# Neighbourhood bias rows repeated in 512-byte pieces, and the repeat moved behind the small loads of block 0

## The chip, the cores and the metric

One core of a Trainium2 chip runs the whole program. Its engines are TensorE (PE in the rows, PEld for its weight loads), VectorE (DVE), ScalarE (ACT), GpSimd (POOL) and SyncE (SP); 16 DMA engines move the data, fed by queues that the engines fill. The metric is device time of one execution in microseconds. Smaller is better.

## What is computed

Two blocks of layers, one after the other, on 256 tokens of width 1024. The first block has two layers: a mixer (latent attention in layer 0, dilated attention with a relative bias in layer 1), a gated feed-forward net and a gated extra term:

```
for i in range(DEPTH):
    hn = rms_norm(h, g[0])
    y = mla_mixer(...)  or  dilated_mixer(..., rel_bias)
    h = h + rms_norm(y, g[1])
    h = h + rms_norm(swiglu(rms_norm(h, g[2]), ffn_w_in[i], ffn_w_out[i]), g[3])
    h = h + (p[i] @ ple_w_proj[i]) * jax.nn.sigmoid(h @ ple_w_gate[i])
```

The second block has two layers with differential attention, spatial gating, neighbourhood attention and a mixture of 32 experts. The neighbourhood attention adds a bias that depends on how far the key's column is from the query's column, read from a small table `na_rpb` of 8 heads x 15 row distances x 31 column distances for each layer:

```
rpb_c = rpb[:, :, dc_idx]            # dc_idx = key column - query column + 15, clipped
bias = jnp.take(rpb_c, dr_idx, axis=1)
s_win = jnp.where(col_ok, s_win + bias, NEG_INF)
```

## The kernel before

All engines run one long program each and meet at semaphores. What matters here is the stretch from about 137 to 470 us: the end of the latent attention of layer 0, its output product, the residual, and the first feed-forward net.

**Weights.** SP streams the weights of every product in chunks of 1 MB (a few are smaller) into `weight_ring`, which has four slots (L46, L535). A chunk is asked for as soon as the PE has finished with the chunk four places ahead of it. In the products of this stretch each chunk is used in two parts: ScalarE writes a rounded copy ("high", L1236), GpSimd subtracts it from the chunk and writes the rest ("low", L1486, `low_parts`), and the PE multiplies with the high part (L672, L673) and then with the low part (L677).

**GpSimd's queue.** GpSimd also issues the small loads, in the order of its program and into one DMA queue (q0 in the rows). `load` (L1448) waits until VectorE has asked (`misc_ask`) and then issues one transfer; `row` loads a row of 1024 gains to all 128 partitions (`broadcast_row`). Four DMAs of constants, two tables and one store of the padded neighbourhood rows to DRAM (`rpb_rows`, L1464, 120 rows of 127 numbers for each layer) come first. After that it waits for the attention's first turned probabilities and then issues

- L1509, which copies each of 48 rows of 384 numbers 128 times from DRAM to DRAM (`rel_rows_repeated`, 6144 pieces of 1536 bytes, for the dilated attention);
- L1511, which copies each of 240 rows of 127 numbers 64 times (`rpb_rows_repeated`, 15360 pieces of 508 bytes). The neighbourhood attention reads it far later, with a row step of one number less than the row's length, so that each query column gets its row shifted by one (L1551 to L1554, 64 loads of 64 KB);
- the gain row of the first residual (`row(I["norm_g"][0, 1])`).

Then comes `close_block(0, ...)`. It waits for `port_free`, makes the low parts of the output product's four chunks, issues the gain row of the second residual and the tokens' extra input `p_t` as soon as VectorE asks for them, waits for `port_free` again and makes the low parts of the feed-forward weights.

**VectorE** copies the product out (L1958), sums squares (L1710), waits for the gain row (`loaded()`), and scales by it and adds to the residual (L1967, L1968). It asks for the next two loads and turns the normed rows for the feed-forward net (L1738 to L1757, L1727, L1728), behind which it frees the port.

Of the kernel before, what the change touches and what calls it, by code (L numbers as in the profile page):

```python
# [21 lines left out]
DEPTH = 2  # L22
# [14 lines left out]

OFF_KA, OFF_VA, OFF_KC, OFF_VC, OFF_QA, OFF_QC, OFF_ZB, OFF_GATE = 0, 512, 1024, 1536, 2048, 2560, 3072, 4096
GRID_W, NA_COLS, NA_H, RPB_R, RPB_C = 64, 16, 8, 15, 31
RPB_W = 2 * GRID_W - 1  # L40

NE, NGRP, EPG, D_EXP = 32, 4, 8, 512
CAP = 64
# [91 lines left out]
def build_program(nc, I, out):  # L135
    ctx = ExitStack()
    with ctx:
# [10 lines left out]
        def sem(name):  # L148
            return ctx.enter_context(nc.semaphore(name))
# [32 lines left out]
        rel_dram = nc.dram_tensor("rel_rows", [DIL_G * DIL_H, BIAS_LEN], F32, kind="Internal").ap()  # L182
        rpb_skew = nc.dram_tensor("rpb_rows_repeated", [DEPTH * NA_H * RPB_R, GRID_W * RPB_W], F32, kind="Internal").ap()
        skew_dram = nc.dram_tensor("rel_rows_repeated", [DIL_G * DIL_H, P * BIAS_LEN], F32, kind="Internal").ap()
        gate_dram = nc.dram_tensor("gate_rows_out", [DEPTH, 4 * D], F32, kind="Internal").ap()
        rpb_dram = nc.dram_tensor("rpb_rows", [DEPTH, NA_H * RPB_R, RPB_W], F32, kind="Internal").ap()

# [31 lines left out]
        def ar(a, n):  # L219
            return A[:, a:a + n]  # L220
# [63 lines left out]
        skew_out, rpb_out = sem("bias_rows_repeated"), sem("rpb_rows_repeated")  # L284
# [1156 lines left out]
        def _(pool):  # L1441
# [3 lines left out]
            def load(dst, src):  # L1445

                pool.wait_ge(misc_ask, seen.next(misc_ask))
                nc.gpsimd.dma_start(dst, src).then_inc(misc_in[loads[0] % 4], 16)  # L1448
                loads[0] += 1

            def row(src, width=D, at=0):
                load(brow[:, at:at + width], src.partition_broadcast(P))
# [10 lines left out]
            for l in range(DEPTH):  # L1463
                nc.gpsimd.dma_start(rpb_dram[l], A[0:NA_H * RPB_R, l * P:l * P + RPB_W]).then_inc(scratch_out, 16)  # L1464

# [12 lines left out]
            def low_parts(g, only=None):  # L1478

                for n, (_, width) in enumerate(g.chunks):  # L1480
                    if only is not None and n not in only:
                        continue
                    for i, (k0, kn) in enumerate(g.groups):
                        c, s = g.first[n] + i, g.first_split[n] + i
                        pool.wait_ge(high_ready, s + 1)
                        nc.gpsimd.tensor_tensor(slot(c, kn, width, ring_r), slot(c, kn, width),  # L1486
                                                high(s, kn, width), ALU.subtract).then_inc(low_ready, 1)

            def after_turn():

                pool.wait_ge(port_free, seen.next(port_free))

            def close_block(i, g_o):
                after_turn()
                low_parts(g_o)
                row(I["norm_g"][i, 3])
                load(ar(PLE, 512).rearrange("p (k t) -> p k t", k=2), I["p_t"][i].rearrange("(k p) t -> p k t", p=P))
                after_turn()
                low_parts(g_ff_in[i])
                low_parts(g_ff_out[i])  # L1500
                if i == 0:
                    row(I["norm_g"][1, 1])
                after_turn()
                low_parts(g_ple_g[i])
# [3 lines left out]

            nc.gpsimd.dma_start(skew_dram.rearrange("r (q m) -> r q m", m=BIAS_LEN),  # L1509
                                rel_dram.unsqueeze(1).broadcast_to([DIL_G * DIL_H, P, BIAS_LEN])).then_inc(skew_out, 16)  # L1510
            nc.gpsimd.dma_start(rpb_skew.rearrange("r (q m) -> r q m", m=RPB_W),  # L1511
                                rpb_dram.rearrange("l r w -> (l r) w").unsqueeze(1).broadcast_to(
                                    [DEPTH * NA_H * RPB_R, GRID_W, RPB_W])).then_inc(rpb_out, 16)
            row(I["norm_g"][0, 1])
            close_block(0, g_mla_o)

            def load_bias(j):
# [10 lines left out]
            for j in range(2, N_PAIRS):  # L1528
                pool.wait_ge(dil_max, 4 * (j - 1))
                load_bias(j)  # L1530
            close_block(1, g_dil_o)

            for layer in range(DEPTH):
# [12 lines left out]
                def load_bias(k):  # L1546
                    j, t = na_steps(layer)[biased[k]]
                    for m in range(2):
                        for half in range(2):
                            row_ = (layer * NA_H + 2 * j + m) * RPB_R + 7 - 2 * t - half  # L1550
                            src = bass.AP(tensor=rpb_skew.tensor, offset=row_ * GRID_W * RPB_W + GRID_W - 1,  # L1551
                                          ap=[[RPB_W - 1, 64], [GRID_W * RPB_W, 4], [1, 64]])
# [109 lines left out]
        def _(dve):  # L1662
# [290 lines left out]
            def copy_product(g, dst):  # L1953

                for n, (_, width) in enumerate(g.chunks):
                    for t in range(g.tiles):
                        bank = product_bank()
                        v(copy(dst(n, t), bank[:, 0:width]), acc_used)  # L1958
# [660 lines left out]
```

## Time and profile before

| | |
|---|---|
| time, median of 3 runs (lowest, highest) | 3733.64 us (3725.2, 3735.14) |
| the profiled execution's own time | 3719.02 us |
| its span | 3717.1 us |
| mean granted TensorE clock | 0.894 |
| PE busy | 2822.0 us, 76% of the span |
| DMA moved | 780.56 MB, mean 210 GB/s |

The span is divided into a chain of work that ended last: each piece of it waited for the one ahead. An engine that is idle beside this chain costs nothing. The fifth to seventh of the page's 40 slices (each 92.9 us) hold the stretch above: the first part of it is the only place there where the PE is nearly idle.

### The profile page before, as it was taken

The numbers are of one execution on the slowest core, as the hardware profiler recorded it, in microseconds if no ns is written. First come the engines' busy times: TensorE is split into PE (matmuls) and PEld (weight loads), VectorE is DVE, ScalarE is ACT, GpSimd is POOL, SyncE is SP. The second block draws the span as 40 slices with busy tenths as digits, with TensorE's granted clock in tenths as the row PEclk, the third lists the DMA queues.
The fourth block names the chain that finished last, engine by engine and source line by source line (L and its number), as shares of the span: only waits on it lengthen the run. The fifth ranks groups of instructions, "written<-read, shape, count | busy, mean of one in ns | idle before, by whom it ended". The sixth has DMA issues, their size and how long they took to land.

```text
span 3717.1 us, 35290 instructions
## 1 busy us (share of the span) xinstructions
PE 2822.0 (76%) x13005; PEld 1777.8 (48%) x13005; DVE 1328.4 (36%) x2530; ACT 763.4 (21%) x973; POOL 1033.1 (28%) x495
## 2 busy tenths in 40 slices
PE   4839979997995886879865777774696875777774
PEld 2628757776774664656651222221574562222221
DVE  2722143444214334732353222223437243222223
ACT  0303322233332112511101111111124211111111
POOL 0028736642872341122101000001262520000000
PEclk8869989999997897989977999997799987999997
DMA  7585548862443351022117999998141436999997
GB/s 283 171 131 172 173 140 288 285 235 80 159 170 103 125 170 65 13 94 90 68 45 269 376 374 375 375 373 297 60 134 56 166 118 242 374 375 371 372 373 259
DMA packets 365899, 780.56 MB, mean 210 GB/s; under 512 B 15076, under 2 KB 16274, under 8 KB 365008
## 3 DMA queue, kind: packets, MB, share of 16 engines
q1 hardware_dynamic: 337312, 669.61, 51.4%
q0 software_dynamic: 28464, 109.29, 9.6%
q8 instruction: 80, 1.31, 0.1%
q14 instruction: 43, 0.35, 0.0%
HBM read 733.52 MB, written 62.56 MB: 214 GB/s over the span
## 4 chain that ended last, share of the span: by engine, by line
PE 54%; DMA 25%; DVE 13%; issue 3%; ACT 1%; another core or an unknown queue 1%; POOL 1%; SPq 0%; DVEq 0%; POOLq 0%; ACTq 0%
PE banks L672 11%; PE banks L673 11%; PE banks L677 10%; DMA weight_ring<-in_moe_w_up 10%; DMA weight_ring<-in_moe_w_down 6%; DMA weight_ring<-in_moe_w_gate 5%; PE banks L1006 5%; PE banks L698 4%; PE banks L1028 4%; PE banks L748 2%; DMA rel_rows<-arena 1%; DVE scaled_rows L1710 1%; DVE arena L1723 1%; PE banks L878 1%
## 5 line engine op out<-in xcount | busy, mean ns | idle before, releaser
L1486 POOL TENSOR_TENSOR weight_ring_r<-weight_ring,weights_high_r 128x2048 fp32r<-128x2048 f32 x124 | 564.1, 4556 | 606.2 <-ACT weights_high_r L1236 442.3
L1006 PE MATMUL banks<-weight_ring,arena 128*64 128x512 f32 x2048 | 521.8, 634 | 210.9 <-DMA weight_ring<-in_moe_w_up 137.7
L672 PE MATMUL banks<-weights_high_r,x_transposed_r 128*128 128x512 f32 x1216 | 496.7, 408 | 50.2 <-DVE x_transposed_r L1728 12.3
L1236 ACT ACTIVATE weights_high_r<-weight_ring 128x2048 fp32r<-128x2048 f32 x124 | 234.2, 1898 | 857.4 <-PE banks L677 510.6
L677 PE MATMUL banks<-weight_ring_r,x_transposed_r 128*128 128x512 f32 x1600 | 389.9, 390 | 2.6 <-POOL weight_ring_r L1486 2.5
L1006 PEld LDWEIGHTS banks<-weight_ring,arena 128*64 128x64 f32 x2048 | 132.3, 140 | 533.2 <-issue 204.3
L1617 POOL DMA_DIRECT2D moe_y<-arena x64 | 34.0, 531 | 1080.8 <-DVE arena L2225 1047.5
L677 PEld LDWEIGHTS banks<-weight_ring_r,x_transposed_r 128*128 128x128 f32 x1600 | 299.8, 188 | 67.6 <-POOL weight_ring_r L1486 5.4
L1486 POOL TENSOR_TENSOR weight_ring_r<-weight_ring,gates_r 128x2048 fp32r<-128x2048 f32 (+1 forms) x60 | 271.2, 4528 | 152.8 <-DVE small L1679 81.2
L1028 PE MATMUL banks<-weight_ring,arena 128*64 128x512 f32 x1024 | 268.1, 659 | 45.5 <-DMA weight_ring<-in_moe_w_down 40.3
L748 PE MATMUL banks<-constants,scaled_rows 128*128 128x128 f32 x594 | 102.9, 334 | 257.7 <-DVE scaled_rows L1738 218.7
L672 PEld LDWEIGHTS banks<-weights_high_r,x_transposed_r 128*128 128x128 f32 x1216 | 237.5, 195 | 119.6 <-issue 28.6
L2207 DVE TENSOR_TENSOR arena<-banks,arena 64x1024 f32<-64x1024 f32 x64 | 77.9, 1217 | 462.7 <-ACT arena L1360 462.7
L1360 ACT ACTIVATE arena<-banks 64x1024 f32<-64x1024 f32 x64 | 65.4, 1022 | 771.0 <-PE banks L1006 771.0
L748 PEld LDWEIGHTS banks<-constants,scaled_rows 128*128 128x128 f32 x594 | 89.6, 174 | 275.1 <-DVE scaled_rows L1738 227.1
L673 PE MATMUL banks<-weights_high_r,arena_r 128*128 128x512 f32 x472 | 188.8, 400 | 0.0
L673 PE MATMUL banks<-weights_high_r,tokens_out_r 128*128 128x512 f32 x448 | 181.0, 404 | 0.0
L672 PE MATMUL banks<-gates_r,x_transposed_r 128*128 128x512 f32 x384 | 157.8, 411 | 18.7 <-DVE x_transposed_r L1728 18.7
L1028 PEld LDWEIGHTS banks<-weight_ring,arena 128*64 128x64 f32 x1024 | 74.6, 150 | 191.6 <-issue 124.6
L673 PE MATMUL banks<-gates_r,x_transposed_r 128*128 128x512 f32 x384 | 155.1, 404 | 0.0
L673 PE MATMUL banks<-weights_high_r,x_transposed_r 128*128 128x512 f32 x384 | 153.4, 399 | 0.0
L698 PE MATMUL banks<-weight_ring,arena 128*128 128x512 f32 x320 | 139.8, 593 | 2.2 <-DVE small L1679 2.2
(323 smaller groups left out, 3690.3 us busy)
## 6 DMA issues: line engine op xcount, KB each, us to landing
weight_ring<-in_moe_w_gate SPq DMA_DIRECT2D x128, 1024.0 KB, 10.4
weight_ring<-in_moe_w_up SPq DMA_DIRECT2D x128, 1024.0 KB, 8.7
weight_ring<-in_moe_w_down SPq DMA_DIRECT2D x128, 1024.0 KB, 10.6
weight_ring<-in_w_in SPq DMA_DIRECT2D x56, 1024.0 KB, 5.0
weight_ring<-in_w_ada SPq DMA_DIRECT2D x48, 1024.0 KB, 7.0
weight_ring<-in_ffn_w_in SPq DMA_DIRECT2D x44, 1024.0 KB, 5.0
weight_ring<-in_dil_w_qkv SPq DMA_DIRECT2D x36, 1024.0 KB, 4.9
weight_ring<-in_ffn_w_out SPq DMA_DIRECT2D x20, 1024.0 KB, 5.0
```

The lines of the kernel that those rows point to most:

```text
L672: nc.tensor.matmul(banks[t][:, 0:width], xh, wh[:, k, :], start=k0 + k == 0, stop=False)
L673: nc.tensor.matmul(banks[t][:, 0:width], xl, wh[:, k, :], start=False, stop=False)
L677: last = nc.tensor.matmul(banks[t][:, 0:width], lhs(k0 + k, t)[0], wl[:, k, :], start=False, stop=k0 + k == g.k_tiles - 1)
L698: last = nc.tensor.matmul(banks[t][:, 0:width], lhs(k0 + k, t), w[:, k, :], start=k0 + k == 0, stop=k0 + k == g.k_tiles - 1)
L748: last = nc.tensor.transpose(bank[0:m, n * P:(n + 1) * P], src, ident)
L878: last = nc.tensor.matmul(ps[6 + n % 2][:, m * 64:m * 64 + 64], na_pT(n, m)[:, k * P:(k + 1) * P], vc[:, k0 + k, 2 * j + m, :], start=k == ...
L1006: last = nc.tensor.matmul(halves(ps[m], kt), x, w[:, k, :], start=kt < 2, stop=kt >= KD - 2)
L1028: last = nc.tensor.matmul(halves(ps[2 + half], k), h, w[:, k, :], start=k < 2, stop=k >= 2)
L1236: nc.scalar.activation(high(s, kn, width), slot(c, kn, width), ACT.Copy).then_inc(high_ready, 1)
L1360: nc.scalar.activation(A[0:CAP, E_UP:E_UP + 2 * BANK], pair[0][CAP:2 * CAP, :], ACT.Copy).then_inc(halves_ready, 1)
L1486: nc.gpsimd.tensor_tensor(slot(c, kn, width, ring_r), slot(c, kn, width), high(s, kn, width), ALU.subtract).then_inc(low_ready, 1)
L2207: tt(A[0:CAP, E_SUM:E_SUM + 2 * BANK], pair[0][0:CAP, :], A[0:CAP, E_UP:E_UP + 2 * BANK], ALU.add).then_inc(summed, 1)
```

## The change

The rows of the neighbourhood table get a length of 128 numbers instead of 127 (the last number is never read), so that a piece has 512 bytes instead of 508, and the DRAM buffers, their strides and the reading step (now 127 numbers) follow from the same constant. The copy itself is no longer issued behind the copy for the dilated attention and ahead of the first gain row; it is issued inside `close_block` of layer 0, behind the second gain row and `p_t`, ahead of the second wait for `port_free`.

```
-RPB_W = 2 * GRID_W - 1
+RPB_W = 2 * GRID_W
...
                 row(I["norm_g"][i, 3])
                 load(ar(PLE, 512).rearrange("p (k t) -> p k t", k=2), I["p_t"][i].rearrange("(k p) t -> p k t", p=P))
+                if i == 0:
+                    nc.gpsimd.dma_start(rpb_skew.rearrange("r (q m) -> r q m", m=RPB_W),
+                                        rpb_dram.rearrange("l r w -> (l r) w").unsqueeze(1).broadcast_to(
+                                            [DEPTH * NA_H * RPB_R, GRID_W, RPB_W])).then_inc(rpb_out, 16)
                 after_turn()
...
                                 rel_dram.unsqueeze(1).broadcast_to([DIL_G * DIL_H, P, BIAS_LEN])).then_inc(skew_out, 16)
-            nc.gpsimd.dma_start(rpb_skew.rearrange("r (q m) -> r q m", m=RPB_W),
-                                rpb_dram.rearrange("l r w -> (l r) w").unsqueeze(1).broadcast_to(
-                                    [DEPTH * NA_H * RPB_R, GRID_W, RPB_W])).then_inc(rpb_out, 16)
             row(I["norm_g"][0, 1])
             close_block(0, g_mla_o)
```

GpSimd's program before, from the store of the dilated rows to the first low parts of the feed-forward weights (DMA is an issue, then destination and source; `norm_g` the gain rows):

```order
L1474 DMA rel_rows<-arena 16x384 x2
L1509 DMA rel_rows_repeated<-rel_rows 6144x1x384 [waits probsT_ready,scratch_out]
L1511 DMA rpb_rows_repeated<-rpb_rows 15360x1x127
L1448 DMA broadcast_row<-in_norm_g 128x1024 [waits misc_asked]
L1486 ISA
L1486 TENSOR_TENSOR weight_ring_r<-weight_ring,weights_high_r 128x2048 [waits weights_high_ready,vector_port_free]
L1486 TENSOR_TENSOR weight_ring_r<-weight_ring,weights_high_r 128x2048 [waits weights_high_ready]
L1486 TENSOR_TENSOR weight_ring_r<-weight_ring,gates_r 128x2048 [waits weights_high_ready] x2
L1448 DMA broadcast_row<-in_norm_g 128x1024 [waits misc_asked]
L1448 DMA arena<-in_p_t 128x2x256 [waits misc_asked]
L1486 TENSOR_TENSOR weight_ring_r<-weight_ring,weights_high_r 128x2048 [waits weights_high_ready,vector_port_free]
```

The same place of the changed kernel:

```order
L1474 DMA rel_rows<-arena 16x384 x2
L1513 DMA rel_rows_repeated<-rel_rows 6144x1x384 [waits probsT_ready,scratch_out]
L1448 DMA broadcast_row<-in_norm_g 128x1024 [waits misc_asked]
L1486 ISA
L1486 TENSOR_TENSOR weight_ring_r<-weight_ring,weights_high_r 128x2048 [waits weights_high_ready,vector_port_free]
L1486 TENSOR_TENSOR weight_ring_r<-weight_ring,weights_high_r 128x2048 [waits weights_high_ready]
L1486 TENSOR_TENSOR weight_ring_r<-weight_ring,gates_r 128x2048 [waits weights_high_ready] x2
L1448 DMA broadcast_row<-in_norm_g 128x1024 [waits misc_asked]
L1448 DMA arena<-in_p_t 128x2x256 [waits misc_asked]
L1499 DMA rpb_rows_repeated<-rpb_rows 15360x1x128
L1486 TENSOR_TENSOR weight_ring_r<-weight_ring,weights_high_r 128x2048 [waits weights_high_ready,vector_port_free]
```

One issue has moved past the first gain row, four low parts and two loads. The other engines' programs are the same in both kernels, except for line numbers.

## Rows read from the trace of the kernel before

**Rows 1.** VectorE's timeline, 212 to 264 us; last column: idle before, and its releaser.

```profile
212.02 0.17 DVE L1715 TENSOR_SCALAR small<-small 128x2 f32<-128x2 f32 x1
212.53 0.17 DVE L1717 RECIPROCAL small<-small 128x2 f32<-128x2 f32 x1 [0.34 <-ACT small L1224]
258.46 1.28 DVE L1967 SCALAR_TENSOR_TENSOR scaled_rows<-tokens_out,small,broadcast_row 128x1024 f32<-128x1024 f32 x1 [45.77 <-DMA broadcast_row<-in_norm_g]
```

**Rows 2.** The chain that ended last, 204 to 266 us: start, length, what.

```profile
206.84 1.83 PE banks L677 x8
...
212.53 0.17 DVE small L1717
212.69 45.66 another core or an unknown queue
...
258.46 1.30 DVE scaled_rows L1967
```

**Rows 3.** GpSimd's timeline, 137 to 296 us.

```profile
137.27 2.13 POOL L1509 DMA_DIRECT2D rel_rows_repeated<-rel_rows  x1 [117.22 <-PE banks L826]
171.73 4.70 POOL L1511 DMA_DIRECT2D rpb_rows_repeated<-rpb_rows  x1 [32.33 <-issue]
176.24 0.82 POOL L1448 DMA_DIRECT2D broadcast_row<-in_norm_g  x1
...
264.01 0.57 POOL L1448 DMA_DIRECT2D broadcast_row<-in_norm_g  x1 [61.57 <-DVE small L1679]
264.57 0.75 POOL L1448 DMA_DIRECT2D arena<-in_p_t  x1
277.33 9.13 POOL L1486 TENSOR_TENSOR weight_ring_r<-weight_ring,weights_high_r 128x2048 fp32r<-128x2048 f32 x2 [12.01 <-DVE small L1679]
...
295.55 4.61 POOL L1486 TENSOR_TENSOR weight_ring_r<-weight_ring,weights_high_r 128x2048 fp32r<-128x2048 f32 x1
```

**Rows 4.** DMA issues of the whole span: KB each, median us from issue to landing.

```profile
weight_ring<-in_ffn_w_in SPq DMA_DIRECT2D x44, 1024.0 KB, 5.0
...
rel_rows_repeated<-rel_rows POOLq DMA_DIRECT2D x1, 9216.0 KB, 33.9
...
rpb_rows_repeated<-rpb_rows POOLq DMA_DIRECT2D x1, 7620.0 KB, 84.6
...
arena<-in_p_t POOLq DMA_DIRECT2D x2, 256.0 KB, 4.5
```

**Rows 5.** Transfers of GpSimd's first gain row and the second: landing min, median, max.

```profile
DMA to landing us min/median/max: 4.4/43.3/82.1
```

**Rows 6.** DMA view, 141 to 171 us (the dilated copy alone): GB/s in 40 parts, queues.

```profile
GB/s 375 381 381 362 356 344 301 338 319 264 332 258 319 283 367 329 301 307 362 338 301 332 307 326 227 283 289 306 301 332 381 369 326 344 307 326 276 221 114 31
DMA packets 2014, 9.24 MB, mean 308 GB/s; under 512 B 16, under 2 KB 16, under 8 KB 2010
```

**Rows 7.** DMA view, 176 to 192.3 us (the 508-byte copy alone).

```profile
GB/s 0 0 56 213 191 258 236 112 112 112 101 101 101 79 79 157 67 135 135 67 112 112 90 112 135 146 90 90 180 45 168 90 101 112 90 123 101 123 135 101
...
q0 software_dynamic: 407, 1.86, 96.5%
```

**Rows 8.** DMA view, 213 to 239 us (that copy beside weights): packets, MB, share.

```profile
q0 software_dynamic: 602, 2.75, 79.1%
q1 hardware_dynamic: 599, 1.19, 24.1%
```

**Rows 9.** SP's timeline: weight chunk issues at 192, 285 and 290 us.

```profile
192.36 24.61 SPq L535 DMA_DIRECT2D weight_ring<-in_ffn_w_in  x4
...
285.07 0.37 SPq L535 DMA_DIRECT2D weight_ring<-in_ffn_w_in  x1
...
290.51 0.37 SPq L535 DMA_DIRECT2D weight_ring<-in_ffn_w_in  x1
```

**Rows 10.** ScalarE's timeline: the high parts of the fifth and sixth chunk.

```profile
290.80 1.91 ACT L1236 ACTIVATE weights_high_r<-weight_ring 128x2048 fp32r<-128x2048 f32 x1
295.56 1.92 ACT L1236 ACTIVATE weights_high_r<-weight_ring 128x2048 fp32r<-128x2048 f32 x1 [2.85 <-DMA weight_ring<-in_ffn_w_in]
```

**Rows 11.** PE's timeline: first product, and the passes over the fifth and sixth chunk's low part.

```profile
277.17 0.80 PE L672 MATMUL banks<-weights_high_r,x_transposed_r 128*128 128x512 f32 x1 [5.57 <-DVE x_transposed_r L1728]
...
305.29 1.98 PE L677 MATMUL banks<-weight_ring_r,x_transposed_r 128*128 128x512 f32 x8
...
310.73 1.98 PE L677 MATMUL banks<-weight_ring_r,x_transposed_r 128*128 128x512 f32 x8
```

**Rows 12.** Windows: length, busy time (count) by engine, granted clock, DMA share, GB/s.

```profile
277.20:281.60 4.40, 4.40 (x10) 3.44 (x11) 0.04 (x1) 0.00 (x0) 4.27 (x1) 0.50 0.00 0
...
349.10:360.50 11.40, 11.40 (x54) 9.43 (x53) 3.10 (x7) 4.49 (x4) 9.22 (x2) 1.00 0.56 183
```

## The prediction

> **What bounds the kernel now.** I read the chain that ended last first, around the place of the change. Between 212.69 and 258.35 us it holds one piece of 45.66 us that no engine's work fills [rows 2]. VectorE's timeline names it: the residual's first multiplication (L1967) starts at 258.46 after 45.77 us of idle time, released by the gain row's transfer [rows 1]. PE, ScalarE and GpSimd have nothing to do in that time. Next, why the row is late: GpSimd issued it at 176.24, right behind the copy of the neighbourhood rows (171.73, 4.70 us to issue) [rows 3]. It needed 82.1 us to land, where the second gain row of the same size needed 4.4 [rows 5]; 176.24 + 82.1 = 258.3. The copy needed 84.6 us and landed at 171.73 + 84.6 = 256.3 [rows 4]. Both are in one queue, and the row came out 2 us behind the copy. So the path is: copy, row, residual. Nobody needs the copy itself before the neighbourhood attention.
>
> **The gain row moves ahead of the copy.** After the change the row follows the dilated copy. GpSimd stood still for 32.33 us between that copy's issue and the next one, with no releaser in the trace, and went on at 171.73, as the dilated copy had landed (137.27 + 33.9 = 171.2) [rows 3, 4]. Whether the small row is held as well, I can't tell; at worst it is issued at 171.7 and lands at about 176, 36 us before VectorE needs it at 212.7. Removed: the whole wait, 45.8 us. What is late next is nothing else: the root that ScalarE gave had ended it the last time (0.34 us of idle time ahead of L1717 [rows 1]), and only the row stands between. All that follows on VectorE, PE and the rings is set by these engines, so I shift it by 45.8 us as it is.
>
> **The copy's issue on GpSimd.** The second gain row and `p_t` come at 264.01 and 264.57, now 218.2 and 218.8; the copy's issue starts at 219.5. Its 4.70 us [rows 3] lie in an idle time of 12.01 us ahead of the low parts at 277.33, now 231.5. If the issue is held until `p_t` has landed (4.5 us [rows 4]), it ends at 228; still free. It is wrong by at most some us if VectorE's work slows the issue. The issue's old place, 171.7 to 176.4, had cover too, so nothing is gained by leaving it. Three more edits cost nothing: the two stores of `rpb_rows` grow by 1 part in 127, the later reads step by 508 instead of 504 bytes with as many pieces as before, and the column of padding is zeroed already.
>
> **How long the copy takes now** decides the rest. It has 15360 pieces. Two rows bound it. By the piece: it moved from about 176 to 256.3 us, 80 us for 960 pieces on each of 16 DMA engines, 83 ns each; the dilated copy moved 384 pieces of 1536 bytes per engine in about 31 us, 81 ns each [rows 4, 6]. If a piece costs that much whatever its size, the new copy takes 80 us as well. By the byte: the dilated copy ran at 308 GB/s [rows 6], so 7.86 MB take some 26 us. I take the byte. The 508-byte copy shows why: in its first 2 us it moved 191 to 258 GB/s, and only then fell to about 110 [rows 7]. The DMA engines can thus process such pieces at more than twice the sustained rate, so I take it that what holds them is how such pieces are written, behind the engines. And the dilated copy starts at 375 to 381 GB/s [rows 6], so its 81 ns are a limit by bytes; that they equal the 83 ns is chance.
>
> The Trainium skill ("DMA: Bandwidth & Descriptors", the table at its head) says that below 512 bytes a transfer's writes become read-modify-write, and from 512 on don't. By it the sum is that by the byte; by the equal cost of a piece in the two copies it would be the other. The rows do not show a piece of 512 bytes, so the case rests on the fall within the copy.
>
> **The copy beside the weights.** This is the new cost. The copy now runs from about 224 us (4.5 us behind its issue, as before: 171.73 to 176) into the first feed-forward product. That starts at 277.17 - 45.8 = 231.4 with four chunks in the ring, issued from 192.36 on as before [rows 9, 11] and now landing unhindered. The fifth chunk is asked for at 285.07 - 45.8 = 239.3. Until then the copy has all DMA engines for 15.3 of its 26 us. From there the queues take turns packet by packet: 602 and 599 packets in 26 us [rows 8]. Before, a packet held nine pieces (2.75 MB / 602 = 4568 bytes), so the copy has some 1707 packets, 107 per DMA engine; at 26 us that is 244 ns each. A weight packet of 2 KB takes 88 ns (599 in 24.1% of 16 x 26 us is 167 ns beside this copy; a chunk of 32 packets per engine that lands in 5.0 us with some 2 us of fixed time gives 90; I take the latter). Together 334 ns for a pair: the fifth chunk takes 10.7 us instead of 2.8 and lands 7.9 us late; the copy ends at about 254 (10.7 us of work left at 239.3, stretched by 334/244), and the sixth chunk lands some 8 us late as well, since it queues behind the fifth.
>
> How late may they be? The fifth chunk's high part was made at 290.80 [rows 10], its low part took 4.6 us, and the PE began with that low part at 305.29 [rows 11]. The high part could start at 305.29 - 4.61 - 1.91 = 298.8, 8 us later; for the sixth 310.73 - 6.52 = 304.2 against 295.56, 8.6 us. So the delay of some 8 us just fits, and GpSimd, whose idle time in this product is about 2 us in 11.4 [rows 12], gets it back in a few chunks. If the copy starts 4 us later or takes 30 us, 2 to 4 us are lost. I put the stall at 0, with 0 to 5 as its range. The clock gives nothing: the PE works at a granted 0.50, the lower level of 1.2 GHz, for the 4.4 us from 277.2 [rows 12], and it stands idle ahead of that in the new kernel too (from 208.7 to about 222).
>
> **Sum.** 3719.0 - 45.8 + 0 = 3673.2 us for an execution like the profiled one, whose span is 3717.1. The median of the runs shown is 14.6 us above that execution; against it I forecast 3733.6 - 45.8 = 3687.8, say 3688.
>
> **Rivals.**
>
> *The pieces stay slow.* 80 us at 83 ns each. For: the equal price of pieces of 508 and 1536 bytes. Against: the fast start [rows 7]. Then 80 - 15.3 = 64.7 us run beside the weights, which got 46 GB/s (1.19 MB in 26 us [rows 8]), 22.9 us for a chunk, where the PE takes one each 5.7 us (two in 11.4 [rows 12]). 2.8 chunks come where 11.4 are wanted: 8.6 x 5.7 = 49 us late, less the 8 us of slack 41. Net gain 5 us: 3729, no difference that can be told.
>
> *Half way.* The copy takes some 50 us, between the two bounds. Nothing in the rows excludes it, since none shows a piece between 508 and 1536 bytes, and nothing speaks for it. Packets of 469 ns, pairs of 557; 34.7 us of work become 41 us, in which 2.3 chunks come instead of 7.2: 28 us late, 20 after the slack. Net gain 26: 3708.
> The Trainium skill ("DMA: Bandwidth & Descriptors", "Latency and other measured facts") lists loads whose rows lie a large power of two apart as slower, down to half at steps of 4 MiB; the new table rows lie 32 KiB apart, and no run here shows such a step. By it the copy could be of this kind.
>
> *Slower than before.* The mechanism is the same starvation of the weight ring, with a copy that is slower than now. The gain is used up where (T - 15.3) x (1 - 5.7/22.9) - 8 = 45.8, at T = 87 us or 91 ns a piece; 11 us more are lost from T = 102. At T = 110 the sum is 63 us of stall, 17 net: 3751. Nothing in the rows speaks for a piece that gets dearer by four bytes more.
>
> *The change doesn't do what it says:* the row is held back by the dilated copy. It can't be for longer than that copy lasts, and that ends 41 us before VectorE wants the row; under 1%, counted with the pieces that stay slow.
>
> **How the numbers follow.** Forecast 72%, half way 12%, pieces stay slow 11%, slower 5%. About 0.3%, 11 us, is what a measurement of this kernel can tell from no change. Faster: 72 + 12 and a little of the third, 85%; same 10%; slower 5%. The range reaches from the forecast with the scatter of the medians (some 5 us either way around 3734, and another 6 us if the clock rises sooner or the run is like the profiled one) to the half-way case: 3676 to 3712. The forecast's own range is 3676 to 3696.
>
> **What would show it.** In the changed kernel VectorE's L1967 follows L1717 within 1 us at about 213, the chain has no unnamed piece there, the first gain row lands in a few us or with the dilated copy, and `rpb_rows_repeated` lands in 30 to 45 us from an issue near 220. ScalarE waits for chunks for at most a few us between 240 and 265, and the PE not at all. If the copy's landing time is near 90 us, the second rival holds and the PE shows gaps at L672 released by high parts that wait for `weight_ring`. The prediction is wrong if the gap at 213 remains under another releaser, or if the feed-forward product takes over 5 us more than now.

## The result and the profile after

The changed kernel takes 3671.99 us (median of 4 runs, 3668.6 to 3678.55), the kernel before 3729.42 us in the same comparison: ratio 0.9848, 95% interval 0.9824 to 0.9872, a gain of 57 us (48 to 66). The forecast was 3688, with a range from 3676: the direction and most of the size are right, but the gain of some 46 us is too small, and the measured time lies 4 us under the range. Of the 15.8 us between forecast and result, 4.2 lie in the kernel before: the forecast started from its median of 3 runs, 3733.6 us, and in this comparison its median is 3729.4. The other 11.6 us are gain that the forecast doesn't hold.

The profiled execution took 3669.42 us with a span of 3667.5, so it is 49.6 us shorter than the one of before. In the page's 40 slices the stretch of interest (137 to 470 us) lies in the second to sixth, not in the fifth to seventh; the PE was busy for 3 tenths of the third slice before and is for 7 tenths of it now. Two gaps thus want an explanation: 49.6 against 45.8 within the traces, and 57 against 49.6 between traces and timed runs.

First VectorE's timeline of the changed kernel (start, length, line, operands; in brackets the idle time before and its releaser), which answers to [rows 1]:

```profile
204.95 0.69 DVE L1959 COPY tokens_out<-banks 128x512 f32<-128x512 f32 x1 [0.21 <-PE banks L677]
...
208.72 0.17 DVE L1718 RECIPROCAL small<-small 128x2 f32<-128x2 f32 x1 [0.34 <-ACT small L1224]
208.92 1.28 DVE L1968 SCALAR_TENSOR_TENSOR scaled_rows<-tokens_out,small,broadcast_row 128x1024 f32<-128x1024 f32 x1
...
216.86 3.81 DVE L1716 TENSOR_SCALAR small<-small 128x2 f32<-128x2 f32 x1
221.01 0.17 DVE L1718 RECIPROCAL small<-small 128x2 f32<-128x2 f32 x1 [0.34 <-ACT small L1224]
```

The wait is gone: the residual's multiplication (now L1968) follows the reciprocal at once. But it starts at 208.92, and 258.46 - 208.92 is 49.5 us, not 45.8. VectorE arrives 3.8 us sooner than it did at 212.53 [rows 1]. Further down an instruction on 128x2 numbers lasts 3.81 us, where the same one lasted 0.17 us before:

```profile
266.41 0.17 DVE L1715 TENSOR_SCALAR small<-small 128x2 f32<-128x2 f32 x1
```

GpSimd's timeline answers to [rows 3]:

```profile
138.68 2.13 POOL L1513 DMA_DIRECT2D rel_rows_repeated<-rel_rows  x1 [118.21 <-PE banks L826]
140.77 0.59 POOL L1448 DMA_DIRECT2D broadcast_row<-in_norm_g  x1
...
215.94 4.74 POOL L1499 DMA_DIRECT2D rpb_rows_repeated<-rpb_rows  x1
231.43 9.10 POOL L1486 TENSOR_TENSOR weight_ring_r<-weight_ring,weights_high_r 128x2048 fp32r<-128x2048 f32 x2 [10.75 <-DVE small L1680]
```

The small row's issue isn't held back by the dilated copy: it comes at 140.77, where the big copy had to stand until 171.73 [rows 3]. The row lands 35.0 us later, at 175.8, just behind the dilated copy (174.6) and long before VectorE wants it. The copy's issue lasts from 215.94 to 220.68, and the stretched instruction of VectorE (216.86 to 220.67) lies inside it and ends with it.

The DMA issues (KB each, us to landing), against [rows 4], and the chain that ended last in the changed kernel:

```profile
rpb_rows_repeated<-rpb_rows POOLq DMA_DIRECT2D x1, 7680.0 KB, 38.1
```

```profile
216.86 3.82 DVE small L1716
...
237.32 1.85 PE banks L677 x8
239.18 15.76 DMA weight_ring<-in_ffn_w_in
254.97 1.92 ACT weights_high_r L1236
256.96 4.62 POOL weight_ring_r L1486
```

The copy lands in 38.1 us instead of 84.6. The new cost is where the forecast had it: the fifth chunk of the feed-forward weights is asked for at 239.18 and takes 15.8 us instead of 5.0 [rows 4]. The PE waits for it twice, 1.0 us for its high and 0.8 us for its low part. ScalarE stands 10.0 us for this chunk, where the forecast had said a few us at most.

### The profile page after: what moved, and what is told of

It reads as the page before. It is cut to its first block, busy times and chain, and to the rows that moved or that the text cites. A ratio compares the mean times of both kernels' runs of the same rounds, so it can differ in the third digit from the quotient of the medians.

```text
span 3667.5 us, 35290 instructions
## 1 busy us (share of the span) xinstructions
PE 2823.1 (77%) x13005; PEld 1778.1 (48%) x13005; DVE 1319.3 (36%) x2530; ACT 763.2 (21%) x973; POOL 1032.3 (28%) x495
## 4 chain that ended last, share of the span: by engine, by line
PE 53%; DMA 26%; DVE 14%; issue 3%; POOL 2%; ACT 2%; SPq 0%; DVEq 0%; POOLq 0%; ACTq 0%
PE banks L672 10%; PE banks L673 10%; PE banks L677 10%; DMA weight_ring<-in_moe_w_up 10%; DMA weight_ring<-in_moe_w_down 7%; DMA weight_ring<-in_moe_w_gate 5%; PE banks L1006 5%; PE banks L698 5%; PE banks L1028 4%; PE banks L748 1%; DMA rel_rows<-arena 1%; DMA weight_ring<-in_dil_w_qkv 1%; POOL weight_ring_r L1486 1%; DVE scaled_rows L1711 1%; DVE arena L1724 1%
## 5 line engine op out<-in xcount | busy, mean ns | idle before, releaser
L748 PE MATMUL banks<-constants,scaled_rows 128*128 128x128 f32 x594 | 104.8, 339 | 209.0 <-DVE scaled_rows L1739 174.6
L2208 DVE TENSOR_TENSOR arena<-banks,arena 64x1024 f32<-64x1024 f32 x64 | 77.9, 1217 | 460.6 <-ACT arena L1360 460.6
L2226 DVE TENSOR_TENSOR arena<-banks,arena 64x1024 f32<-64x1024 f32 x64 | 77.9, 1217 | 182.6 <-ACT arena L1374 182.6
## 6 DMA issues: line engine op xcount, KB each, us to landing
weight_ring<-in_moe_w_gate SPq DMA_DIRECT2D x128, 1024.0 KB, 10.4
weight_ring<-in_moe_w_down SPq DMA_DIRECT2D x128, 1024.0 KB, 10.6
```

The source lines that it names most:

```text
L748: last = nc.tensor.transpose(bank[0:m, n * P:(n + 1) * P], src, ident)
L2208: tt(A[0:CAP, E_SUM:E_SUM + 2 * BANK], pair[0][0:CAP, :], A[0:CAP, E_UP:E_UP + 2 * BANK], ALU.add).then_inc(summed, 1)
L2226: tt(A[0:CAP, E_Y + par * D:E_Y + (par + 1) * D], pair[1][0:CAP, :], A[0:CAP, E_YR:E_YR + D], ALU.add).then_inc(y_ready, 1)
```

## Experiments

All were built from the two kernels; the differences are given against the kernel named.

**The move alone.** The changed kernel with rows of 127 numbers.

```
-RPB_W = 2 * GRID_W
+RPB_W = 2 * GRID_W - 1
```

> The copy is issued at its new place, but with pieces of 508 bytes as before. The forecast's own arithmetic (rival 'the pieces stay slow'): the copy lands some 80 us behind its issue near 216, runs 65 us beside the first feed-forward product and gives weights only 46 GB/s there; the PE waits for chunks, 35 to 45 us in sum, so the kernel gains 0 to 15 us on before (ratio 0.996 to 1.000). The rival reading, that weights beside the copy are not starved because the queue of SP gets more than one packet for each of the copy's once more chunks are open: a gain of 35 us or more (ratio under 0.991).

Measured: 3716.82 us (median of 12 runs) against 3727.39 (17 runs), ratio 0.9972 (0.9959 to 0.9985), a gain of 10.6 us, within the first expectation. The copy landed 86.4 us behind its issue. The PE's waits in the feed-forward product and the queues' packets from 241 to 290 us (queue, packets, MB, share of 16 DMA engines):

```profile
PE banks L672 <- ACT weights_high_r L1236: 40.6, 2, 24.0
```

```profile
q0 software_dynamic: 1039, 4.75, 79.3%
q1 hardware_dynamic: 842, 1.69, 22.4%
```

1.69 MB of weights in 49 us is 34 GB/s, less than the 46 of [rows 8], because in the first 8 us the weights' queue moved no packet at all (the copy's moved 186); from 257 to 290 us the two moved 682 and 681. So moving a slow copy gives most of the wait back as waits for weights: the forecast's rival "the pieces stay slow", with the 41 us that it had worked out. The product as a whole lasts 127 us instead of 82, 45 more: beside the waits it loses 4 to 5 us, with the clock at a granted 0.59 from 280 to 286 us, behind the first of them.

**The size alone.** The kernel before with rows of 128 numbers.

```
-RPB_W = 2 * GRID_W - 1
+RPB_W = 2 * GRID_W
```

> The copy stays where it was, ahead of the first gain row, with pieces of 512 bytes. In the changed kernel it landed 38.1 us behind its issue. If the piece's size alone sets that, it lands at 171.7 + 38 = 210 and the row at about 212, just when VectorE asks for it (212.7): the wait of 45.8 us shrinks to 0 to 3 us and this kernel gains 43 to 50 us (ratio 0.987 to 0.9885), nearly all of what both parts give together. If the move is what makes the copy fast (other traffic, another neighbour in the queue), the copy still takes 80 us here and nothing is gained (ratio 1.00).

Measured: 3677.91 us (5 runs), ratio 0.9862 (0.9839 to 0.9884), a gain of 49.5 us. VectorE's timeline there:

```profile
208.34 0.17 DVE L1717 RECIPROCAL small<-small 128x2 f32<-128x2 f32 x1 [0.34 <-ACT small L1224]
216.86 1.28 DVE L1967 SCALAR_TENSOR_TENSOR scaled_rows<-tokens_out,small,broadcast_row 128x1024 f32<-128x1024 f32 x1 [8.35 <-DMA broadcast_row<-in_norm_g]
```

The copy landed 40.9 us behind an issue at 173.86 that came 2 us later than expected, and VectorE arrived at 208.5 instead of 212.7; hence a wait of 8.35 us and not of 0 to 3. The piece's size gives most of the change's worth by itself; in the same comparison the changed kernel, with the move as well, is a further 9.7 us faster (3668.25).

**The changed kernel and the kernel before, again.** No edit. There are two more traces and two more comparisons of the changed kernel, two more traces of the kernel before and one comparison of it with itself.

> The changed kernel itself once more, for a closer ratio. If the forecast's sum is right and the first comparison's 57 us was its scatter, the gain is 45 to 51 us (ratio 0.9863 to 0.988; the two profiled spans differ by 49.6 us). If there is a second gain that the forecast doesn't hold, it stays at 54 to 60 us (ratio 0.984 to 0.9855).

> The kernel before once more, for its trace. Its first profiled execution took 3719.0 us, 8 us less than the median of its 17 timed runs (3727.4), while the changed kernel's two profiled executions (3669.4, 3668.3) lie at its median (3668.3). If that first profile was simply a quick run, this one takes 3722 to 3735 us and is behind the first one in the second block's stages (from 1100 us on), while the stretch up to 900 us agrees within 2 us. In that stretch VectorE's copy of 128x1024 at L1740, near 172 us, should again last some 5 us beside GpSimd's issue of the copy (171.7), where it lasts 1.4 us in the changed kernel. If it starts ahead of the issue, as in the run with the new piece size alone, it lasts 1.4 us and this run is 4 us quicker there.

> The kernel before against itself. It shows what a comparison of this kernel can tell, and gives a third trace. In the second trace the wait for the gain row was 55.1 us, against 45.8 in the first, because VectorE came to it 3.8 us earlier (no instruction stretched beside the issue) and the copy landed 5.6 us later. If the first trace was the odd one, the wait is 52 to 57 us here again and L1740 lasts 1.4 us. If both forms are common, it is anything from 45 to 56. Ratio 0.997 to 1.003, both ways, if the timed runs are fair; the 8 us by which two profiled executions lay under the timed median should then be seen in this kernel's own times too or go.

> The changed kernel against before in the same call, for a third trace and ratio. If the gain is the wait of 52 to 57 us less 3.7 us for the stretched instruction (L1716) and 1 to 3 us for the weights, it is 46 to 52 us, ratio 0.986 to 0.9877. If the two earlier comparisons (57 and 59 us) are right, something of 6 to 10 us is gained that the traces of before don't show in their first 900 us: ratio 0.984 to 0.9855.

Measured for the changed kernel: 3668.25 us, ratio 0.9847 (0.9825 to 0.9869), and 3671.18 us, ratio 0.983 (0.9814 to 0.9845). The kernel before against itself: ratio 1.0 (0.9989 to 1.0012), so nothing but the kernel makes the difference; its medians in these comparisons are 3727.39 and 3731.36 us. The last ratio of the changed kernel, 0.983, lies beyond both of the ranges expected for it. The further profiled executions of before took 3718.41 and 3733.22 us. The expectation that the second would be 3722 us or more missed, and so did the one that the stretch up to 900 us agrees within 2 us: the second trace was 5.8 us behind the first at 359 us and level with it again by 900.

These are VectorE's rows in the second trace of before (the copy L1740 at 173, the wait at 264), and GpSimd's issue in it:

```profile
173.20 1.42 DVE L1740 COPY scaled_rows<-tokens_out 128x1024 f32<-128x1024 f32 x2
...
263.99 1.28 DVE L1967 SCALAR_TENSOR_TENSOR scaled_rows<-tokens_out,small,broadcast_row 128x1024 f32<-128x1024 f32 x1 [55.08 <-DMA broadcast_row<-in_norm_g]
```

```profile
173.76 5.15 POOL L1511 DMA_DIRECT2D rpb_rows_repeated<-rpb_rows  x1 [33.23 <-issue]
```

and in the third:

```profile
268.18 1.28 DVE L1967 SCALAR_TENSOR_TENSOR scaled_rows<-tokens_out,small,broadcast_row 128x1024 f32<-128x1024 f32 x1 [60.17 <-DMA broadcast_row<-in_norm_g]
```

```profile
rpb_rows_repeated<-rpb_rows POOLq DMA_DIRECT2D x1, 7620.0 KB, 92.6
```

and this is the first trace, on which the forecast rested:

```profile
172.08 5.59 DVE L1740 COPY scaled_rows<-tokens_out 128x1024 f32<-128x1024 f32 x2
```

So the removed wait was 45.8, 55.1 and 60.2 us in three executions of one kernel; the second and third lie in and above the 52 to 57 us expected. Two ends set it. The gain row came 5.5 and 9.7 us later than in the first trace: the copy ahead of it was issued 2.0 and 1.8 us later, and needed 88.2 and 92.6 us to land instead of 84.6. And VectorE arrived 3.8 and 4.7 us earlier, because in the first trace alone two engines collided: GpSimd began its issue at 171.73, VectorE its 128x1024 copies at 172.08, and these then lasted 5.59 us instead of 1.42. In the other two VectorE was ahead of the issue and was not touched; there the issue lasted 5.15 and 4.91 us instead of 4.70. The first trace had both the shortest copy and a VectorE that arrived 4 us late, so it showed the smallest wait of the three.

**The copy's issue earlier.** The changed kernel, with the issue behind the output product's low parts, where VectorE is idle.

```
                 low_parts(g_o)
+                if i == 0:
+                    nc.gpsimd.dma_start(rpb_skew..., rpb_dram...)
                 row(I["norm_g"][i, 3])
                 load(ar(PLE, 512)..., I["p_t"][i]...)
-                if i == 0:
-                    nc.gpsimd.dma_start(rpb_skew..., rpb_dram...)
                 after_turn()
```

> The changed kernel with the copy's issue one step earlier: behind the low parts of the output product (about 199.7) and ahead of the second gain row, where VectorE is idle until 204 and the weight ring is being refilled. Two things should go: the 3.8 us by which one short VectorE instruction is stretched while GpSimd writes the copy's descriptors (216.9 in the changed kernel), and most of the 2.2 us for which the PE waits for the fifth chunk. So 4 to 6 us below the changed kernel (ratio to before 0.9833 to 0.9867). If the stretched instruction has nothing to do with GpSimd's issue, it stays where it is, and the kernel gains at most 2 us on the changed one.

> The kernel with the earlier issue once more, beside the changed kernel on the same chip. In its first trace it was 3 to 5 us ahead of the changed kernel at 360 us (no stretched instruction, no wait for weights), but its timed median was 1.6 us behind. If the 3 to 5 us are real and not given back, its median is 2 to 6 us under the changed kernel's in this call; if the later stages give them back, within 2 us.

Measured: 3669.88 us, ratio 0.9853 (0.9832 to 0.9874), and in the later comparison 3669.93 us, ratio 0.9827 (0.9813 to 0.9841), beside 3668.25 and 3671.18 for the changed kernel in the same comparisons; the 4 to 6 us expected on the changed kernel are missed. The mechanism works: the instruction that was stretched lasts 0.17 us again, with no issue beside it,

```profile
217.19 0.17 DVE L1716 TENSOR_SCALAR small<-small 128x2 f32<-128x2 f32 x1
```

and the PE no longer waits for weights in the feed-forward product. At 359 us two traces of this kernel are 4.8 and 5.7 us ahead of the mean of three of the changed kernel (48.85 and 49.80 us ahead of the first trace of before, against 43.5, 45.8 and 42.8). In the traces the lead lasts to the end (3664.24 and 3665.80 us for the profiled executions, 3668.25 to 3671.18 for the changed kernel's). In the timed medians nothing of it is left: 1.6 us behind in one comparison and 1.3 us ahead in the other. I can't tell it from no change, and why the medians don't show those 5 us is open.

**What makes a piece slow.** Three kernels with another piece, each otherwise the changed kernel. First 508 bytes in slots of 512:

```
-nc.gpsimd.dma_start(rpb_skew.rearrange("r (q m) -> r q m", m=RPB_W),
-                    rpb_dram.rearrange("l r w -> (l r) w").unsqueeze(1).broadcast_to(
-                        [DEPTH * NA_H * RPB_R, GRID_W, RPB_W])).then_inc(rpb_out, 16)
+nc.gpsimd.dma_start(rpb_skew.rearrange("r (q m) -> r q m", m=RPB_W)[:, :, 0:RPB_W - 1],
+                    rpb_dram.rearrange("l r w -> (l r) w")[:, 0:RPB_W - 1].unsqueeze(1).broadcast_to(
+                        [DEPTH * NA_H * RPB_R, GRID_W, RPB_W - 1])).then_inc(rpb_out, 16)
```

> The changed kernel, but each piece copies only 127 of the 128 numbers: pieces of 508 bytes that all begin on a multiple of 512 bytes, in the source and in the destination. If what made the old copy slow is that a write of under 512 bytes is partial, it stays slow: landing 75 to 90 us. If it was the odd starting address of each piece, the copy is quick: landing 36 to 42 us.

Then rows of 129 numbers (`RPB_W = 2 * GRID_W + 1`) and of 144 numbers (`2 * GRID_W + 16`), with the staging columns of the second layer's table at 112 instead of 128:

> The changed kernel with rows of 129 numbers: pieces of 516 bytes, over 512, but none of them (apart from each 128th) begins on a multiple of 512 or 64 bytes. The small table's staging columns are moved to make room. If only the size counts, the copy lands in 36 to 42 us. If the ends that fall inside a unit of memory are what costs, it stays slow, 75 to 95 us, and the first feed-forward product waits some 40 us for its weights.

> The changed kernel with rows of 144 numbers: pieces of 576 bytes, all beginning on a multiple of 64 bytes, only each eighth on a multiple of 512. If whole units of 64 bytes are enough, the copy runs by its bytes: 8.85 MB at some 308 GB/s, 29 us, plus 8 to 10: landing 38 to 44 us. If it takes a larger unit (256 or 512 bytes), it stays slow, 75 us or more, or comes out between as the 508-byte pieces in 512-byte slots did (57 us).

From 223 to 236 us the copy is alone on the DMA engines in all of them. One line per kernel, in the order 512 (the changed kernel), 508 (the move alone), 508 in slots, 516, 576 bytes; the last two numbers are the DMA share and GB/s:

```profile
223.00:236.00 13.00, 7.43 (x24) 6.01 (x23) 7.30 (x13) 6.39 (x4) 4.57 (x2) 0.64 0.99 294
```

```profile
223.00:236.00 13.00, 7.43 (x26) 6.16 (x25) 7.70 (x14) 7.04 (x5) 3.93 (x1) 0.63 1.05 113
```

```profile
223.00:236.00 13.00, 7.43 (x24) 6.03 (x23) 7.30 (x13) 6.33 (x4) 4.64 (x2) 0.50 1.04 156
```

```profile
223.00:236.00 13.00, 7.43 (x25) 6.07 (x24) 7.30 (x13) 6.60 (x4) 4.37 (x1) 0.63 1.02 106
```

```profile
223.00:236.00 13.00, 7.43 (x26) 6.20 (x26) 7.76 (x14) 7.11 (x5) 3.87 (x1) 0.63 1.00 279
```

Landing took 38.1, 86.4, 57.1, 88.0 and 46.3 us; the last is 2 us more than expected. The three new kernels have one execution each: 3688.62 (508 in slots), 3712.07 (516) and 3678.52 us (576). Neither of my two readings of the slot kernel holds by itself: it came out between them. Pieces of 516 bytes end to end, so that nearly all of them begin and end inside a unit of 64 bytes, are as slow as those of 508 (106 against 113 GB/s), so the length is not what matters alone. Pieces of 508 bytes that each begin on a multiple of 512 are quicker (156) but not quick. 576 bytes that begin and end on multiples of 64 run at 279 GB/s, nearly like 512 at 294, though only one in eight begins on a multiple of 512.

The rule of the Trainium skill that was weighed in the forecast ("DMA: Bandwidth & Descriptors", table at its head: full rate from 512 bytes on) gave the right side for this change; the 516-byte kernel, at 106 GB/s, speaks against it as the only condition.

What fits all five is that pieces must cover whole units of 64 bytes or fewer. It also fits all five that a piece must have 512 bytes or more and begin on such a unit: the slot kernel is both under 512 bytes and cut inside a unit, and no kernel has a piece that is short but whole (448 bytes, say). How large the unit is (64, 32 or 16 bytes) wasn't tried either, nor which side, reading or writing, pays.

**The row first, the copy in its old place.** The kernel before with two statements swapped.

```
+            row(I["norm_g"][0, 1])
             nc.gpsimd.dma_start(rpb_skew..., rpb_dram...).then_inc(rpb_out, 16)
-            row(I["norm_g"][0, 1])
```

> The kernel before with the first gain row ahead of the copy; the copy stays near 172 us, with pieces of 508 bytes. The wait of 45.8 us at 212.7 goes. But the copy runs from 176 to about 256 beside the first four weight chunks (asked for from 192 on), which get 46 GB/s: about one chunk per 23 us, so near 215, 237, 252 and 259, where the feed-forward product, now starting at 231, wants the third at about 236 (for its high part) and the fourth at 241. The PE waits 10 to 20 us there; a gain of 27 to 37 us on before (ratio 0.990 to 0.993). If the weights are not starved by the copy, the gain is 45 us or more (ratio under 0.988).

Measured: 3697.56 us (4 runs) against 3724.22, ratio 0.9923 (0.9905 to 0.9941), a gain of 27 us, at the lower end of what was expected; the copy landed 88.9 us behind its issue. The PE waited for high parts of the weights:

```profile
PE banks L672 <- ACT weights_high_r L1236: 15.6, 1, 15.6
PE banks L672 <- ACT gates_r L1236: 7.5, 1, 7.5
```

23 us, more than the 10 to 20 expected: ScalarE had the four chunks at 227, 251, 267 and 270 us, not at 215, 237, 252 and 259. The product also began 2 us late, for its first chunk, and lasted 110 us instead of 82, so the whole loss is some 30 us; the PE worked at a granted 0.50 from 253 to 258 us, behind the longer of the waits. With the move alone this makes a pair: a slow copy costs 30 us where it begins before the ring is filled, and 45 where it begins behind.

## Why the prediction was right or wrong

**The path was right.** The gain row behind the copy in one queue was what the residual waited for. With the row ahead, the residual's multiplication starts at once in all three traces of the changed kernel (208.92, 208.20 and 206.82 us, each 0.03 us behind the reciprocal).

**The size of the wait was wrong, and it is the step that failed.** "Removed: the whole wait, 45.8 us" took the length of the wait in one execution for what the change removes. The wait is a difference of two times: when the row lands, and when VectorE arrives. Both are different in other executions: 45.8, 55.1, 60.2 us, mean 53.7. "The median of the runs shown is 14.6 us above that execution; against it I forecast 3733.6 - 45.8" treated that distance as something that both kernels have. The changed kernel doesn't have it: its three profiled executions (3669.42, 3668.25, 3671.18) lie within 3 us of its medians. Whether the distance belonged to the wait is not shown. The second execution of before was as quick as the first in total (3718.41 against 3719.02) with a wait that was 9.3 us longer: it was 5.8 us behind at 359 us and made that up before 900. What the traces do show is that one of them doesn't give the length of this wait to better than some 8 us.

**The old place of the issue was not free in that execution.** "The issue's old place had cover too, so nothing is gained by leaving it" is wrong there: VectorE's copies at 172.08 lasted 5.59 us instead of 1.42, and the PE, which waited for them, was then at a granted 0.54 from 184 to 190 us, where in the changed kernel it was at 0.95 on the same product; VectorE, which had been 1.4 us ahead of the changed kernel before the copies, came to the residual 3.8 us later than there. In that execution this cost nothing, since the gain row came later still; it only made the wait look shorter. The row was in the profile ("4.98 us issue" in the chain at 172), beside an issue of 4.70 us, and I didn't put the two together. That is the difference between the 45.8 us of the forecast and the 49.5 by which L1968 moved between the first two traces.

**The new place costs nearly the same again.** I allowed for GpSimd being slowed by VectorE; it is the other way round. L1716 on the path takes 3.81 us instead of 0.17, in all three traces of the changed kernel. I had put 0.

**The copy's time was right.** 26 us by the byte at 308 GB/s; it ran at 294 GB/s while alone, and landed in 38.1, 35.9 and 39.6 us, within the 30 to 45 given. The bound by the piece (80 us) fell, by the size alone (40.9 us to landing in the old place). The reason given was right in part: a piece's bytes set its time only where its ends are whole, as the 516-byte kernel shows. Nothing came of the "half way" case: with rows 32 KiB apart in the new table the copy ran at 294 GB/s.

**The weights beside the copy were nearly right.** Forecast: the fifth chunk 7.9 us late, 8 us of slack, a stall of 0, range 0 to 5. Measured: 10.8 us late in the first trace, and the product 2.4 us longer (84.4 us instead of 82.0, counted from its first multiplication to 359 us in the trace of before). In the other two traces it lasted 82.8 and 87.2 us, in those of before 82.3 and 82.7, so the mean loss is 2.5 us. The step that was off is "From there the queues take turns packet by packet". They do, but not from there: from 240 to 244 us, right behind the chunk's issue, the copy's queue moved 281 packets and the weights' 26,

```profile
q0 software_dynamic: 281, 1.15, 99.8%
q1 hardware_dynamic: 26, 0.05, 3.5%
```

and only from 244 to 248 us 194 and 195. Those first us are about what the chunk was later than forecast. (A slip besides: 3.0 us for 32 packets are 94 ns each, not 90 or 88. It changes nothing.) With the slow piece the same arithmetic gave 41 us against 40.6 us of PE waits; since the product as a whole lost 45, that agreement is partly luck.

**The sum with the measured terms.** Over the first 359 us, where the traces can be laid side by side: the three executions of before stand at 0, +5.8 and +10.4 us relative to the first, those of the changed kernel at -43.5, -45.8 and -42.8. The means differ by 49.5 us. The terms are 53.7 of wait, plus 1.9 because VectorE reaches the residual at 208.0 on average instead of 209.9 (the collision at 172, in one of three, and scatter), less 3.6 for L1716 and 2.5 for weights: 49.4.

Over the whole span the means are +4.5 and -49.4, so 54 us. Of the 4 to 5 us behind 359 us, 3.5 have a place, and "All that follows ... I shift it by 45.8 us as it is" is wrong there: near 1424 us a VectorE instruction (L2370) lasts 3.80 us beside GpSimd's masks in the first trace of before and 0.71 at the same place of the changed kernel's,

```profile
1423.69 3.80 DVE L2370 TENSOR_SCALAR scaled_rows<-scaled_rows 128x512 f32<-128x512 f32 x1
```

```profile
1376.94 0.71 DVE L2371 TENSOR_SCALAR scaled_rows<-scaled_rows 128x512 f32<-128x512 f32 x1
```

and this is not scatter. It lasts 0.71 or 0.72 us in every trace with the issue at the changed kernel's place, whatever the piece (seven traces), and 3.79 to 3.81 in every trace with the old place or the earlier one (seven too). Why the two engines meet otherwise there was not tried.

The timed medians say 57, 59 and 60 us. The intervals of the first two comparisons (48 to 66 and 49 to 65) hold the 54, that of the third (58 to 69) doesn't. The remaining 3 to 6 us I leave open: three traces of a wait that scatters over 14 us can't settle it.

## What to carry to other kernels

A wait read from one profiled execution is a sample. Where its end is a slow transfer, take a second and a third before the range is set; the execution's total time doesn't tell whether its wait was short or long (55.1 us of wait in 3718.4, 45.8 in 3719.0). Look for what a transfer is queued behind before asking how long it takes itself; and move a slow transfer only after making it fast, since beside a weight stream it cost 30 or 45 us of the 54 that it had cost before. Before a big issue on GpSimd is moved, see what VectorE does at both places.

## What the runs showed of the hardware

- While GpSimd issued the copy of 15360 pieces (4.7 us), VectorE instructions that began in that time stood until about its end: two copies of 128x1024 between SBUF tiles took 5.59 us instead of 1.42, an operation on 128x2 numbers 3.81 instead of 0.17. Not all did: a read of VectorE's accumulator took its usual 0.08 us (at 216.75 in the changed kernel), and operations with an input in PSUM went on at 0.69 us each beside the issue, in the kernel with the new size alone (issue 173.86 to 179.07). Where VectorE's copies had begun first, they kept their 1.42 us and the issue lasted 4.91 to 5.21 us (three traces).
- The Trainium skill ("SBUF — State Buffer", "Who interferes with whom") tells of one port pair that the two share as an exclusive lock: whichever starts first keeps it and the other blocks. Its examples are mostly of VectorE holding up GpSimd's descriptors. The durations above agree with the rule; on the critical path here it was GpSimd that held up VectorE (3.81 us instead of 0.17). That the port pair is the cause wasn't tried.
- In all five traces with the old place, GpSimd's issue of the 15360 pieces stood 32 to 34 us behind the issue of the dilated copy's 6144 pieces, until these had landed; the issue of a row of 128 pieces at the same place did not stand at all.
- A DRAM-to-DRAM copy of 15360 pieces, alone on the DMA engines, ran at 106 to 113 GB/s with 516 or 508 bytes end to end, at 156 with 508 bytes that each begin on a multiple of 512, at 279 to 294 with 576 or 512 bytes that cover whole units of 64 bytes.
- Once both queues moved packets, they moved about as many each: 602 and 599 beside the slow copy [rows 8], 727 and 720 from 196 to 208 us beside the fast one in its old place. That left the weights 46 GB/s (1.19 MB in 26 us) beside the slow copy and 120 GB/s (1.44 MB in 12 us) beside the fast one, in the kernel with the new size alone:

```profile
q0 software_dynamic: 727, 2.97, 66.3%
q1 hardware_dynamic: 720, 1.44, 35.1%
```

- A chunk of weights that was asked for while the copy had the DMA engines to itself got few packets or none at first: 26 in 4 us beside the fast copy, none in 8 us beside the slow one (issue at 240.15 in the kernel with the move alone, and at 192.36 in the kernel before).
